# Second norm of a two-layer hybrid diffusion step: modulation rows turned at the end of attention, shift and row scaling joined on DVE

## The reference, cut to what matters

```python
shift1, scale1, gate1, shift2, scale2, gate2 = adaln(cond, w_ada, b_ada)
x  = x + gate1 * (merged @ w_out)
h2 = rms_norm(x, norm2_g) * (1 + scale2) + shift2      # the second norm
x  = x + gate2 * hier_moe(h2)                          # router, then experts
```

## Time and profile before

| what | value |
|---|---|
| median of three runs | 1949.23 us |
| the profiled execution, own time | 1945.07 us |
| its span | 1943.2 us |
| mean granted TensorE clock | 0.919 |
| PE busy | 1672.5 us (86%) |
| DVE busy | 1220.6 us (63%) |
| ACT busy | 904.7 us (47%) |
| POOL busy | 430.2 us (22%) |

### The profile page before, as it was taken

The page is one execution under the profiler, slowest core; times in us unless marked ns, Lnnn a source line. Parts: engine busy times, 40 slices in busy tenths (PEclk is TensorE's granted clock), DMA queues, the critical chain, the costliest instruction groups (busy, mean ns, idle before and its releaser), DMA issues.

```text
span 1943.2 us, 34341 instructions
## 1 busy us (share of the span) xinstructions
PE 1672.5 (86%) x13277; PEld 1120.0 (58%) x13277; DVE 1220.6 (63%) x1888; ACT 904.7 (47%) x1478; POOL 430.2 (22%) x274
## 2 busy tenths in 40 slices
PE   6799889999989894888879998999999999398876
PEld 4478766666665453443466886666666555243435
DVE  4595355776637537877675926476773573677754
ACT  3322555666541124767532235465664211367753
POOL 0032251111131204212102324211112221321202
PEclk7899999999999896999859998999999999699995
DMA  8555235422236456999644722321123544299964
GB/s 291 178 195 166 73 137 198 156 98 67 93 117 232 178 192 216 349 378 365 231 175 147 239 72 90 100 96 60 55 72 125 201 151 151 93 353 366 375 224 166
DMA packets 191106, 350.71 MB, mean 180 GB/s; under 512 B 15477, under 2 KB 98934, under 8 KB 190710
## 3 DMA queue, kind: packets, MB, share of 16 engines
q1 hardware_dynamic: 181647, 319.58, 47.2%
q0 software_dynamic: 7776, 28.32, 3.9%
q10 hardware_dynamic: 1543, 0.88, 0.2%
HBM read 287.72 MB, written 61.01 MB: 179 GB/s over the span
## 4 chain that ended last, share of the span: by engine, by line
PE 62%; DVE 13%; DMA 10%; ACT 6%; issue 5%; DVEq 2%; SPq 1%; POOL 0%; ACTq 0%; POOLq 0%
PE PS L430 36%; PE PS L437 10%; DMA arena<-in_moe_w 4%; DMA wf<-in_moe_w 3%; PE PS L1033 3%; PE PS L1049 3%; PE PS L851 2%; DVE arena L2369 2%; PE PS L807 1%; DMA wf<-in_w_out 1%; PE PS L833 1%; PE PS L817 1%; DVE ostat L2205 1%; ACT arena L1615 1%; ACT arena L1433 1%
## 5 line engine op out<-in xcount | busy, mean ns | idle before, releaser
L1719 POOL TENSOR_TENSOR wlo<-wf,whi 128x1024 f16<-128x1024 f32 x112 | 250.6, 2258 | 974.2 <-ACT whi L1360 974.2
L430 PE MATMUL PS<-hpart,whi 128*128 128x320 f16 x2048 | 431.7, 304 | 16.9 <-ACT arena L1433 15.9
L430 PE MATMUL PS<-hpart,wlo 128*128 128x320 f16 x1024 | 310.6, 303 | 0.0
L430 PE MATMUL PS<-whi,hpart 128*128 128x256 f16 (+2 forms) x1568 | 297.0, 290 | 5.9 <-DVE scratch L1989 3.6
L430 PEld LDWEIGHTS PS<-hpart,whi 128*128 128x128 f16 x2048 | 193.1, 99 | 110.5 <-issue 35.1
L430 PE MATMUL PS<-wlo,hpart 128*128 128x256 f16 (+2 forms) x784 | 225.0, 289 | 0.0
L430 PEld LDWEIGHTS PS<-whi,hpart 128*128 128x128 f16 x1568 | 151.6, 98 | 64.4 <-issue 22.9
L2369 DVE TENSOR_TENSOR arena<-arena 128x2048 f16<-128x2048 f32 x66 | 149.5, 2288 | 42.0 <-ACT arena L1615 41.9
L2165 DVE TENSOR_REDUCE stat<-PS 128x1 f32<-128x640 f32 (+1 forms) x160 | 110.7, 713 | 99.0 <-PE PS L1033 96.7
L1433 ACT ACTIVATE arena<-PS,pcol 128x320 f32<-128x320 f32 x128 | 67.5, 527 | 179.1 <-PE PS L430 173.9
L1999 DVE SCALAR_TENSOR_TENSOR scratch<-scratch,cw 128x655 f32<-128x655 f32 x120 | 138.8, 1198 | 4.8 <-issue 0.4
(11 more groups left out here) (351 smaller groups left out, 2899.9 us busy)
## 6 DMA issues: line engine op xcount, KB each, us to landing
arena<-in_moe_w SPq DMA_DIRECT2D x66, 1024.0 KB, 9.3
arena<-in_w_ada SPq DMA_DIRECT2D x40, 1024.0 KB, 8.1
wf<-in_moe_w SPq DMA_DIRECT2D x36, 1024.0 KB, 9.9
wf<-in_w_gate SPq DMA_DIRECT2D x32, 1024.0 KB, 5.5
g_rows<-arena SPq DMA_DIRECT2D x128, 160.0 KB, 1.8
wf<-in_w_in SPq DMA_DIRECT2D x18, 1024.0 KB, 7.7
y_rows<-scratch SPq DMA_DIRECT2D x34, 512.0 KB, 9.0
arena<-g_rows SPq DMA_DIRECT2D x24, 640.0 KB, 5.1
```

Of the source, the lines that this page charges most:

```text
L430: ins = pe.matmul(out, st, mv, start=first and n == 0, stop=last and n == 2)
L1719: ins = pool.tensor_tensor(lo[:, a:b], wf[j][:, a:b], hi[:, a:b], ALU.subtract)
```

## The change

The columns are laid side by side by DVE in step g = 48 (the step behind the last head), turned by PE ahead of the last gate half, and copied out by DVE ahead of its last `wo_low`. SP writes `mod_rows` at h = 4 of the gate loads. The broadcasts are read back as soon as the 16th multiplication is done. The gain rows have a semaphore of their own. ACT's scaling and POOL's addition are replaced by one DVE instruction for a tile (two for tile 0): three tiles behind `hot_ready`, two behind `place_ready`. Three of the five first loads of expert weights no longer wait for `w_lo(l, V_ALL)`.

```diff
 SP
+                    if h == 4:
+                        sp.wait_ge(*mrow_ready(l, 1))
+                        sp.dma_start(mod_rows[0:1, 0:4096]..., mrow).then_inc(mod_out.sem, 16)
+                        sp.dma_start(mod_rows[0:1, 4096:4136]..., brow).then_inc(mod_out.sem, 16)
                     gates_load(h)
...
-                sp.wait_ge(*mrow_ready(l, 1))
-                sp.dma_start(mod_rows[0:1, 0:4096]..., mrow).then_inc(mod_out.sem, 16)
-                sp.dma_start(mod_rows[0:1, 4096:4136]..., brow).then_inc(mod_out.sem, 16)
                 sp.wait_ge(*mod_out(l, 2 * 16))
-                for dst, a, b in ((arena[:, 6144:8192], 0, 2048), (scratch[:, 4040:4080], 4096, 4136),
+                sp.wait_ge(*m_used(l, 2 * KC))
+                sp.dma_start(arena[:, 6144:8192], mod_rows[0:1, 0:2048].partition_broadcast(P)).then_inc(gain_in.sem, 16)
+                for dst, a, b in ((scratch[:, 4040:4080], 4096, 4136),
                                   (shrow0[0], 2048, 2592), (shrow0[1], 2592, 3072), (shrow, 3072, 4096)):
...
+                for j, q in ((0, 2), (1, 0), (1, 1)):
+                    load(slice(j, j + 1), j, q)
                 sp.wait_ge(*w_lo(l, V_ALL))
-                for j, q in ((0, 0), (0, 1), (0, 2), (1, 0), (1, 1)):
-                    load(slice(j, j + 1), j, q)
+                for q in range(2):
+                    load(slice(0, 1), 0, q)
 PE
+                pe.wait_ge(*ex_ready(l, TILES * MAPS))
+                pe.wait_ge(*mcol_ready(l, 1))
+                pe.wait_ge(*wr_in(l, 4 * 16))
+                pe.transpose(bank(0)[0:32, 0:P], mcol, ident[:, :])
+                for k in range(KC):
+                    pe.matmul(bank(1)[0:2, 0:20], ada[:, 24 + k, :], wr[:, k, :], start=k == 0, stop=False)
+                pe.matmul(bank(1)[0:2, 0:20], ones[0:20, 0:2], rb20, start=False, stop=True).then_inc(mod_done.sem, 1)
                 for i in GATE_SETS[HEADS_ALL + 4]:
                     gate_set(i)
                 pe.wait_ge(*z_split(l, 1))
-                pe.wait_ge(*ex_ready(l, TILES * MAPS))
+                pe.wait_ge(*mrow_ready(l, 1))
...
-                pe.wait_ge(*m_used(l, 2 * KC))
...
 ACT
-                act.wait_ge(*dg_ready(l, 2))
-                for tile in range(TILES):
-                    act.mul(htok[:, tile, :], xraw[:, tile, :], stat[:, 1, tile:tile + 1]).then_inc(tmp_ready.sem, 1)
...
-                act.wait_ge(*rows_scaled(l, TILES))
                 for c in range(2):
                     for q in range(3 - c):
+                        if (c, q) == (0, 2):
+                            act.wait_ge(*rows_whole(l, TILES))
                         part_high(c, c, 0, q, True)
 POOL
-                for tile in range(TILES):
-                    pool.wait_ge(*rows_scaled(l, tile + 1))
...
-                        ins = pool.tensor_tensor(htok[:, tile, :], htok[:, tile, :], shrow, ALU.add)
-                    ins.then_inc(hf_ready.sem, 1)
 DVE
+                dve.wait_ge(*mod_done(l, 1))
+                dve.tensor_copy(mrow, bank(0)[0:32, 0:P])
+                dve.tensor_copy(brow, bank(1)[0:2, 0:20]).then_inc(mrow_ready.sem, 1)
                 wo_low(1)
...
-                        dve.wait_ge(*mod_in(l, 5 * 16))
+                        dve.wait_ge(*gain_in(l, 16))
...
+                dve.wait_ge(*mod_in(l, 4 * 16))
                 dve.tensor_tensor(route[:, 0, :], route[:, 0, :], lbase[:, 0, :], ALU.add)
...
+                def row_tile(tile):
+
+                    for dst, row in (((0, 544), shrow0[0]), ((544, D), shrow0[1])) if tile == 0 else (((0, D), shrow),):
+                        ins = dve.scalar_tensor_tensor(out=htok[:, tile, dst[0]:dst[1]], in0=xraw[:, tile, dst[0]:dst[1]],
+                                                       scalar=stat[:, 1, tile:tile + 1], in1=row, op0=ALU.mult, op1=ALU.add)
+                    ins.then_inc(hf_ready.sem, 1)
...
                 dve.tensor_tensor(cum, ohm[:, 0:5, :], ohm[:, 5:10, :], ALU.add).then_inc(hot_ready.sem, 1)
+                for tile in range(3):
+                    row_tile(tile)
                 dve.wait_ge(*cnt_done(l, 1))
...
                 ins.then_inc(place_ready.sem, 1)
+                for tile in range(3, TILES):
+                    row_tile(tile)
...
-                dve.wait_ge(*rows_whole(l, TILES))
                 part_low(0, 0, 1)
```

More of the change, by code:

```diff
@@ L299, in build @@
         params_in = sig("params_in", 17 * 16)
-        wr_in = sig("wr_in", 11 * 16)
-        mod_out, mod_in = Signal(wr_in.sem, 11 * 16, 4 * 16), Signal(wr_in.sem, 11 * 16, 6 * 16)
+        wr_in = sig("wr_in", 10 * 16)
+        mod_out, mod_in = Signal(wr_in.sem, 10 * 16, 4 * 16), Signal(wr_in.sem, 10 * 16, 6 * 16)
+        gain_in = sig("gain_in", 16)
         cache_in = sig("cache_in", 9 * 16)
@@ L329, in build @@
         rn_done = sig("rn_done", 1)
-        tmp_ready = sig("tmp_ready", KC + TILES)
+        tmp_ready = sig("tmp_ready", KC)
         hf_ready = sig("hf_ready", KC + TILES)
-        rows_scaled, rows_whole = (Signal(v.sem, KC + TILES, KC) for v in (tmp_ready, hf_ready))
+        rows_whole = Signal(hf_ready.sem, KC + TILES, KC)
         h_ready = sig("h_ready", 8)
@@ L674, in _ @@
                         sp.wait_ge(*m_used(l, h - 3))
+                    if h == 4:
+                        sp.wait_ge(*mrow_ready(l, 1))
+                        sp.dma_start(mod_rows[0:1, 0:4096].rearrange("o (r n) -> (o r) n", r=32), mrow).then_inc(mod_out.sem, 16)
+                        sp.dma_start(mod_rows[0:1, 4096:4136].rearrange("o (r n) -> (o r) n", r=2), brow).then_inc(mod_out.sem, 16)
                     gates_load(h)
@@ L1113, in _ @@
                 ahead = l + 1 < LAYERS
-                pe.wait_ge(*m_used(l, 2 * KC))
-                pe.wait_ge(*mcol_ready(l, 1))
-                pe.wait_ge(*wr_in(l, 4 * 16))
-                pe.transpose(bank(4)[0:32, 0:P], mcol, ident[:, :])
-                for k in range(KC):
-                    pe.matmul(bank(5)[0:2, 0:20], ada[:, 24 + k, :], wr[:, k, :], start=k == 0, stop=False)
-                pe.matmul(bank(5)[0:2, 0:20], ones[0:20, 0:2], rb20, start=False, stop=True).then_inc(mod_done.sem, 1)
                 for u in range(OUT_UNITS):
@@ L1757, in _ @@
                     low(l * V_ALL + (V_OUT + u + 1), u % 2)
-                for tile in range(TILES):
-                    pool.wait_ge(*rows_scaled(l, tile + 1))
-                    if tile == 0:
-                        pool.tensor_tensor(htok[:, 0, 0:544], htok[:, 0, 0:544], shrow0[0], ALU.add)
-                        ins = pool.tensor_tensor(htok[:, 0, 544:D], htok[:, 0, 544:D], shrow0[1], ALU.add)
-                    else:
-                        ins = pool.tensor_tensor(htok[:, tile, :], htok[:, tile, :], shrow, ALU.add)
-                    ins.then_inc(hf_ready.sem, 1)
                 pool.wait_ge(*base_ready(l, 1))
@@ L2254, in _ @@
                             sums(g)
+                    if g == HEADS_ALL:
+                        dve.wait_ge(*wr_in(l, 4 * 16))
+                        cols32 = mcol.rearrange("p (q s k) -> p q s k", q=2, s=2)
+                        dve.tensor_copy(cols32[:, 0], gs[:, 1, :, :].rearrange("p k s -> p s k"))
+                        dve.tensor_copy(cols32[:, 1], ada[:, 24:32, :].rearrange("p k s -> p s k"))
+                        dve.tensor_scalar(rb20, ident[0:20, 0:20], rbias[:, 0:1], None, ALU.mult).then_inc(mcol_ready.sem, 1)
                     if g > HEADS_ALL:
                         wo_low((2, 3, 0)[g - HEADS_ALL - 1])
+                dve.wait_ge(*mod_done(l, 1))
+                dve.tensor_copy(mrow, bank(0)[0:32, 0:P])
+                dve.tensor_copy(brow, bank(1)[0:2, 0:20]).then_inc(mrow_ready.sem, 1)
                 wo_low(1)
@@ L2278, in split @@
                                              op0=ALU.mult, op1=ALU.subtract).then_inc(m_split.sem, 1)
-                dve.wait_ge(*wr_in(l, 4 * 16))
-                cols32 = mcol.rearrange("p (q s k) -> p q s k", q=2, s=2)
-                dve.tensor_copy(cols32[:, 0], gs[:, 1, :, :].rearrange("p k s -> p s k"))
-                dve.tensor_copy(cols32[:, 1], ada[:, 24:32, :].rearrange("p k s -> p s k"))
-                dve.tensor_scalar(rb20, ident[0:20, 0:20], rbias[:, 0:1], None, ALU.mult).then_inc(mcol_ready.sem, 1)
                 for d in range(KC):
@@ L2312, in _ @@
                     dve.tensor_copy(scp[l + 1][:, :, 0:2], scf[:, :, :]).then_inc(cond_wide.sem, 1)
-                dve.wait_ge(*mod_done(l, 1))
-                dve.tensor_copy(mrow, bank(4)[0:32, 0:P])
-                dve.tensor_copy(brow, bank(5)[0:2, 0:20]).then_inc(mrow_ready.sem, 1)
                 def weights_ahead(k):
```

2 lines of the change are left out of this document (removed).

## The result

Over 20 runs of each kernel, taken together, the kernel before has a median of 1945.93 us and the changed one 1929.9 us, from 1921.55 to 1945.57. The ratio is 0.9928, 95% interval 0.9902 to 0.9955: **faster by 14 us, between 9 and 19**.

A forecast was written before the change was run, and what follows sets the result against it. PE led the engine shares and the chain of waits; in the edited stretches PE, DVE and ACT alternate. Terms of +0.5 us in L0 and -7.3 in L1 gave -6.8, from 1949.23 to 1942.4 us, range 1932 to 1950 (8 in 10).

The forecast's parts named there:

- Step 1: Columns turned before the last gate half: costs 0.1 us a layer, 0.8 without cover by PE's idle time.
- Step 2, L0: w_out unit 2 load in L0: issued 6.9 us earlier, landing still later than block 1, gain 6.9 us.
- Step 2, L1: w_out load in L1: reads 6.4 us earlier, landing 2.1 us longer from loads behind, gain 4.3 us.
- Step 3: PE's clock behind the w_out stall: less idleness restores clock, gaining 1.5 us in L0, 0.5 in L1.
- Steps 4 and 5: Routing: without POOL's additions DVE regains 8.6 us (L0), 8.3 (L1); row tiles on DVE cost 3.9, then 2.6.
- Step 6: L0 behind the root: eighth w_ada load goes out behind the fifth row write, delaying PE; loss 8.8 us.
- The first rival: L0's loss is partly made up in the expert loop, where weight loads need only route_ready; 18%.
- Step 7: L1 behind the root, without that w_ada load: route_ready 3.1 us earlier, gather 0.8 late; gain 2.6 us.
- That `w_out` lands as late as now: Broadcasts or other transfers, not its issue, set the w_out landing; total up to +6.4 us; 10%.
- That POOL is not what slows DVE: Routing: DVE's short operations stay slow and the row tiles come on top; +10.1 us in total; 5%.
- The ring order: Loads behind w_out unit 2 do not delay its landing: 2.1 us more gained in L1; 12%.

The follow-up runs named there:

- before_2: The kernel before, unchanged, run and profiled again: 1948.88 us, ratio 1.0003.
- before_3: The kernel before, unchanged, one execution for its profile alone: 1932.38 us.
- weights_wait: Changed kernel with the three expert loads back behind the wait for w_out's low halves: 1933.32 us, ratio 0.9922.
- out_loads_first: Kernel before with only the loads of w_out units 2 and 3 moved ahead of the modulation rows: 1927.33 us, ratio 0.9897.
- best: Changed kernel with the eighth w_ada load ahead of row writes, ada_keep ahead of three casts, w_out units 2 and 3 ahead of modulation rows: 1916.51 us.
- columns_alone: Changed kernel with ACT's scaling and POOL's additions put back: 1926.89 us, ratio 0.9894.
- after_2: The changed kernel, unchanged, run and profiled again: 1933.92 us, ratio 0.9921.
- eighth_early: Changed kernel with the eighth w_ada load moved on SP ahead of the five row writes: 1920.29 us, ratio 0.986.
- rows_alone: Kernel before with only the row tiles on DVE, without ACT's scaling and POOL's additions: 1952.75 us, ratio 1.0033.
- no_additions: Kernel before with POOL's additions of the shift left out, so its results differ: 1922.12 us, ratio 0.9881.
- eighth_early_keep: Changed kernel with the eighth w_ada load ahead of the row writes and ACT's ada_keep ahead of the three casts: 1923.15 us, ratio 0.9894.

## Why the prediction was half right

**Step 1, +0.1 us a layer: nothing to see.** In L0, from PE's last matmul of one gate half to the first of the last half it takes 1.01 us in both kernels (585.85 to 586.86 before, 585.13 to 586.14 after, with the turn between), so the cover held. The sixteenth multiplication ends at 644.25 and 639.63 us after, and at 644.97, 639.72 and 639.45 before.

**Step 2, L0, -6.9: the shift of the issue was right, the landing better.** The load went out 6.85 us earlier against the sixteenth multiplication. But it landed 10.9 us behind its issue, not 12.11, at 657.5, and block 1 was done at 657.8, as forecast (658). The cast came 7.8 us earlier: 0.9 us more. So the sentence that the landing remains the later one failed, by 0.3 us: block 1 sets the cast. And PE's stall ahead of its second turn, which was to be near 3 us, is 1.44 us.

**Step 2, L1, -4.3: too little by 1.3, and half of it right for a wrong reason.** The reads moved by 6.3 us against two of the three profiles of before, as worked out (6.4), and by 7.9 us against before_2. But between the first read and the load SP needed 3.35 us in L1 before (1594.11 to 1597.46; 2.28 and 3.70 in before_2 and before_3) and 2.27 us after, so that the issue moved 7.7 us in the mean. These rows were at hand: I moved the reads and left out the gap behind them. The 2.1 us of longer landing came true to the tenth (mean issue to cast 10.2 before, 12.3 after), and that was luck, for weights_wait shows that the loads behind are not its cause. The Trainium skill, "DMA: Bandwidth & Descriptors", section "Queues, rings and completion order", has the descriptors of a ring consumed in the order of the ring. For the loads behind, weights_wait agrees (0.5 us at most). The 6.4 us that were taken from this for L1 were still wrong, since 2 MB of broadcasts stand ahead in the same queue. Counted from the first read, the load of L1 landed after 13.1 to 13.3 us in all three profiles of before, though the gap to its own issue differed by 1.4 us. In L0 before it was 14.4 us, and after it was 13.2 in L0 and 14.7 in L1. Ahead of the broadcasts it landed 6.5 to 7.8 us from its own issue, and unit 3 after 5.2 to 5.8 (out_loads_first, best). That the broadcasts ahead are the cause fits all of these. None of the runs took them away alone, and why the count from the first read differs by 1.5 us between layers and kernels stays open.

**Step 3, the clock, -1.5 and -0.5: too little, by 1.2 and 0.8.** This was bounded rather than worked out, and in L0 the upper bound was near the truth. The stretch from the cast to the root is 60.5 to 60.8 us in three profiles before, and 57.9 to 58.0 in every profile in which unit 2 came in time, out_loads_first, weights_wait and columns_alone among them: 2.7 us. The window behind the stall went from 0.75 to 1.00. In L1 the stretch took 55.7, 57.1 and 55.7 us before and 54.1 and 55.7 after. PE's window 1608 to 1620 there had granted clocks of 0.86, 0.60 and 0.86 before and of 1.00 and 0.86 after, in the same order as the times. The length of the stall alone does not decide it (second turn of L1 in the timelines of PE, after, then after_2):

```profile
1611.00 1.53 PE L823 MATMUL PS<-scratch,xT 128*128 128x148 f32 x10 [2.68 <-DVE xT L2301]
```

```profile
1613.78 2.83 PE L823 MATMUL PS<-scratch,xT 128*128 128x148 f32 x10 [2.35 <-DVE xT L2301]
```

The longer wait kept the full clock and the shorter did not. What decides between the two, these traces don't show.

**Steps 4 and 5: right.** DVE's short operations all take 0.18 to 0.23 us; three row tiles took 3.80 us and two 2.48 us, where 3.9 and 2.6 were forecast.

**Step 6, L0, +8.8: right, +8.1 and +8.3 measured.** Each link is in the profile: load issued 25.0 us behind the root (25.5 forecast), landed 6.0 us later, half of `ada_unit`, the copy, the casts for 5.50 us, `ada_keep`, 2.3 us, `busy(6)`. The casts followed `ada_copy`; the row tiles, done since 740.3, did not hold them. eighth_early gives back 9.0 us by moving the load alone. The first rival, that L0's loss is partly made up behind, is not borne out: in rows_alone +6.4 was measured with +7.2 traced (an interval that alone would still admit it), and taking the loss away in eighth_early gave 13 us more than the change, not less than 9.

**Step 7, L1, -2.6: -3.3 measured.** `route_ready` came 3.6 us earlier against the root (3.1 forecast), and the gather 0.7 us late against it (0.8 forecast).

**The other rivals.** That `w_out` lands as late as now is refuted by the landings. Its mechanism, that the broadcasts set the landing and not the issue of the load, is nearer to what the runs show than step 2 was: the load came earlier because the broadcasts did. That POOL is not what slows DVE is refuted by no_additions. The ring order was half right, as told above.

**The sum.** From the sixteenth multiplication on, the steps gave +0.4 in L0 and -7.4 in L1; the traces show -2.3 and -10.3. Of the 5.6 us between, 2.2 lie in step 2 (0.9 and 1.3), 2.0 in step 3, 1.4 in steps 6 and 7. So the steps that failed are 2 and 3, by the size of their terms: -6.9 and -4.3 for the loads, which measured -7.8 and -5.6, and -1.5 and -0.5 for the clock, which measured -2.7 and -1.3. L0's term of step 2 stood at the top of its bounds and was still too small, L1's stood at the cautious end, and those of step 3 at a half and a third; all four fell the same way. With -12.6 the forecast would have been 1936.6 for the median shown, and a range of the same width around it would have held the time. Of the 12.5 us between 1942.4 and 1929.9, 5.7 lie in the terms (with step 1's, of which nothing is seen), and 3.3 in the median before, which came out lower over 20 runs than over the first three. The last 3.5 are in neither: the two medians lie 16.0 us apart, where the stretches show 12.6 and the ratio makes it 14.

**What stays open.** The measured gain is larger than the traced one for the change (14 and 15 against 12.6), and so it is in most runs: columns_alone 21 against 19, eighth_early 27 against 23, out_loads_first 20 against 12, no_additions 23 against 16, weights_wait 15 against 12, best 31 against 26; but eighth_early_keep 21 against 26, and rows_alone +6.4 against +7.2. Only out_loads_first leaves its interval, by half a microsecond, and kernels measured together share their runs of before. Three stretches lie outside the table, the expert loops among them, and all vary by themselves. From the start to the sixteenth multiplication of L0 it took 639.5 to 645.0 us before, 639.6 and 644.3 after. From the first turned rows of L0 to the sixteenth multiplication of L1 it took 822.0, 827.7 and 825.1 us in the three profiles of the kernel before, 828.3 and 836.2 in those of the changed one, and 817.4 to 833.9 in the others. From the first turned rows of L1 to the end of the span it took 244.2, 245.6 and 234.7 us before, 251.5 and 243.8 after, 244.4 in eighth_early, 247.5 in weights_wait, and 231.2 to 235.2 in the other six. Whether an edit makes the short form more likely, one profile of each can't say.

## What to carry to other kernels

Follow a moved step along every queue that it shares: the loss of 8 us behind the root in L0 came from a load that nobody edited, standing behind a write that now came later, and moving that one line gave the 9 us back. A load that the chain waits for belongs ahead of bulky reads that are wanted later: issued in front of 2 MB of broadcasts the load of unit 2 landed in 6.5 to 7.8 us, behind them in 9.4 to 12.4. An engine's own order counts beside it: turning the columns early let PE go on without a stop, and that was 3.5 us more. When single executions of a kernel lie 28 us apart, compare stretches between milestones of several profiles, not spans.

## What the runs showed of the hardware

DVE's operations are not slowed alike by POOL's additions. Beside them, TENSOR_TENSOR on 20 elements took 1.97 to 2.23 us, while TENSOR_REDUCE between them, with one input, kept its 0.17 us (timeline of DVE in L0, the kernel before):

```profile
731.26 2.23 DVE L2383 TENSOR_TENSOR wuhi<-wuhi,tie 128x20 f32<-128x20 f32 x1
733.56 0.17 DVE L2385 TENSOR_REDUCE wuhi<-wuhi 128x5 f32<-128x20 f32 x1
```

The Trainium skill, "SBUF — State Buffer", section "Who interferes with whom", says that a DVE instruction with two SBUF inputs contends with a GpSimd instruction that reads SBUF, and that one with at most one SBUF input, outside the 2-port modes, does not. The traces agree: each slowed operation ends within 0.1 us of the end of a POOL addition (2.3 us each), and without these additions (no_additions) they take 0.18 us. The five row tiles on DVE cost less together, 6.3 us, than the waits that they do away with.

PE's idle time ahead of its second turn in L0 was 7.43 us before, up to 671.83, and the granted clock of the next window was 0.75; with 1.44 us of idleness, after and in out_loads_first, it stayed at 1.00. Of the two levels, 1.2 and 2.4 GHz, the window of 12 us at 0.75 spent half its time at either. In between the same wait went both ways: 1.88 us ahead of L1117 was followed by full clock in L0 of the first profile of before and in rows_alone, and by 0.72 in the 6 us from 648 to 654 of out_loads_first.
